# The second layer's gate/up projection as seven half-size products per block, with GpSimd forming the weight sums

## The reference

```python
D_FF = 2816
def conv_ffn(h, w_in, conv_w, conv_b, w_out):
    z = h @ w_in                                   # (512, 1024) @ (1024, 5632)
    g = dwconv(z[..., :D_FF], conv_w, conv_b)      # width 3 along the tokens
    return (jax.nn.silu(g) * z[..., D_FF:]) @ w_out
```

## Time and profile before

| | us |
|---|---|
| median of 3 runs | 1748.97 |
| span of the profiled execution | 1744.6 |
| TensorE busy | 1699.8 (97%), 9234 matmuls |
| VectorE busy | 1102.7 (63%) |
| ScalarE busy | 683.5 (39%) |
| GpSimd busy | 195.1 (11%) |
| granted TensorE clock, mean | 0.997 |

### The profile page before, as it was taken

The page is one execution under the profiler, slowest core; times in us unless marked ns, Lnnn a source line. Parts: engine busy times, 40 slices in busy tenths (PEclk is TensorE's granted clock), DMA queues, the critical chain, the costliest instruction groups (busy, mean ns, idle before and its releaser), DMA issues.

```text
span 1744.6 us, 23609 instructions
## 1 busy us (share of the span) xinstructions
PE 1699.8 (97%) x9234; PEld 1454.8 (83%) x9234; DVE 1102.7 (63%) x1745; ACT 683.5 (39%) x1127; POOL 195.1 (11%) x201
## 2 busy tenths in 40 slices
PE   6999999999999999999999999999999999999998
PEld 4788899787988888888888898879887888888777
DVE  5676777767676766644344678978875644444454
ACT  4343266544422221223344444454455422223442
POOL 1078500002100000000000210111210200000000
PEclk9999999999999999999999999999999999999999
DMA  8633000131334345441312122200012222222321
GB/s 343 215 124 116 17 22 1 75 143 49 133 128 162 138 152 193 169 134 55 114 50 95 40 102 80 97 1 1 33 42 86 95 73 96 97 97 97 131 98 71
DMA packets 40769, 173.08 MB, mean 99 GB/s; under 512 B 12640, under 2 KB 13152, under 8 KB 26208
## 3 DMA queue, kind: packets, MB, share of 16 engines
q1 hardware_dynamic: 31984, 166.75, 26.5%
q10 hardware_dynamic: 8688, 4.99, 1.0%
HBM read 169.60 MB, written 2.13 MB: 98 GB/s over the span
## 4 chain that ended last, share of the span: by engine, by line
PE 87%; DVE 4%; ACT 3%; DVEq 2%; issue 1%; DMA 1%; POOL 1%; ACTq 0%; SPq 0%; another core or an unknown queue 0%
PE PS L297 14%; PE PS L293 14%; PE PS L301 14%; PE PS L608 8%; PE PS L614 8%; PE PS L611 8%; PE PS L1120 4%; PE PS L325 3%; PE PS L328 3%; PE PS L329 3%; PE PS L1105 2%; DMA mod_raw<-modw 1%; DVE w_lo L282 1%; DVEq L1165 1%; ACT w_hi L276 1%
## 5 line engine op out<-in xcount | busy, mean ns | idle before, releaser
L293 PE MATMUL PS<-HT,w_hi 128*128 128x512 f32 (+1 forms) x1248 | 375.6, 347 | 0.0
L297 PE MATMUL PS<-HT,w_hi 128*128 128x512 f32 (+1 forms) x1248 | 375.5, 347 | 0.0
L301 PE MATMUL PS<-HT,w_lo 128*128 128x512 f32 (+1 forms) x1248 | 372.1, 344 | 0.0
L282 DVE TENSOR_TENSOR w_lo<-w_raw,w_hi 128x2048 fp32r<-128x2048 f32 x100 | 231.4, 2314 | 168.4 <-ACT w_hi L276 162.3
L608 PE MATMUL PS<-w_hi,a_ring 128*128 128x512 f32 x670 | 262.8, 392 | 2.9 <-DVE w_lo L282 0.9
L611 PE MATMUL PS<-w_lo,a_ring 128*128 128x512 f32 x670 | 260.9, 389 | 0.0
L276 ACT ACTIVATE w_hi<-w_raw 128x2048 fp32r<-128x2048 f32 x99 | 188.9, 1908 | 160.9 <-PE PS L608 103.7
L301 PEld LDWEIGHTS PS<-HT,w_lo 128*128 128x128 f32 x1248 | 211.7, 189 | 31.9
L293 PEld LDWEIGHTS PS<-HT,w_hi 128*128 128x128 f32 x1248 | 209.5, 188 | 29.9
L297 PEld LDWEIGHTS PS<-HT,w_hi 128*128 128x128 f32 x1248 | 210.6, 189 | 28.5
L988 DVE SCALAR_TENSOR_TENSOR yb<-PS,cws,yb 128x511 f32<-128x511 f32 (+1 forms) x132 | 83.1, 658 | 155.4 <-ACTq L949 151.0
(11 more groups left out here) (321 smaller groups left out, 2660.0 us busy)
## 6 DMA issues: line engine op xcount, KB each, us to landing
w_raw<-wpack SPq DMA_DIRECT2D x102, 1024.0 KB, 4.8
m_raw<-modu SPq DMA_DIRECT2D x80, 512.0 KB, 4.3
mod_raw<-modw SPq DMA_DIRECT2D x8, 1024.0 KB, 11.7
c_rows<-c_scratch SPq DMA_DIRECT2D x6, 512.0 KB, 5.2
X<-x SPq DMA_DIRECT2D x2, 1024.0 KB, 6.5
out<-X SPq DMA_DIRECT2D x4, 512.0 KB, 2.6
X<-ctx SPq DMA_DIRECT2D x1, 1024.0 KB, 10.0
gmB<-gate_rows_evo ACTq DMA_DIRECT2D x1, 1024.0 KB, 4.5
```

The source lines that it names most:

```text
L282: nc.vector.tensor_tensor(w_lo[r][:, :], w_raw[r][:, :], w_hi[r][:, :].bitcast(F32), ALU.subtract).then_inc(wl_ready, 1)
L293: mm = nc.tensor.matmul(o, wh, xh, start=start, stop=False)
L297: mm = nc.tensor.matmul(o, wh, xl, start=False, stop=False)
L301: last = nc.tensor.matmul(o, wl, xh, start=False, stop=stop)
```

## The change

The projection's slots 2 to 21 are computed by a Strassen scheme (seven products in place of eight). The weights of a slot are seen as a 2x2 block matrix: gate and up tile (m) by even and odd feature tiles (k), each block 4 feature tiles of 128 x 128, so 512 elements a partition. The activations are a 2x2 block matrix too: even and odd feature tiles by the first and second half (128) of each token group of 256. A product multiplies one weight matrix with one activation matrix, 4 feature tiles x 3 matmuls of 256 columns. Three products use a raw weight block (`RAW_OF`), four use a sum of blocks (`SUM_OF`), and so do the activations.

- GpSimd forms the four weight sums of each slot, `Sw0` to `Sw3`, from `w_raw` (`form_sum`).
- ScalarE makes the seven high parts `FH0` to `FH6` (`form_hi`), VectorE the seven low parts `FL0` to `FL6` (`form_lo`), 512 elements each. They lie where `w_hi` and `w_lo` lay, one buffer for each product, so that a high part waits for the same product of the slot before.
- The four activation sums ("turned") are formed once in each token group, for group 0 by GpSimd and for group 1 by VectorE (`turned_sum`), and split like the others (`TH`, `TL`). They are formed in place of the scaled activations, which for this norm now have 16 tiles of their own (`h_pre3`) in place of a ring of 6.
- Products share PSUM halves: products 3 and 6 accumulate onto product 0's bank "x" and product 4 onto product 1's bank "y". ScalarE copies out what must be kept before (`seven_keep`: p1, p5, u2, p4, in that order), and TensorE waits for p1 before product 3, p5 before product 4 and u2 before product 6.
- VectorE adds what was kept to what is in PSUM: gate sum `Gf`, up sum `up`. The convolution then reads `Gf` in SBUF and not PSUM.
- The loops over slots are unrolled, some semaphores are merged, and the output projection ffo1 uses banks 4 to 7.

The diff, cut to the new functions that matter here:

```diff
+        SUM_OF = {1: 0, 3: 1, 4: 2, 6: 3}
+        RAW_OF = {0: (0, 0), 2: (1, 0), 5: (1, 1)}
+        TURNED = (0, 2, 1, 3)
+        SPLIT = (0, 2, 1, 3, 4, 5, 6)
+        def formed(s, i):
+            return 6 * s + SPLIT.index(i) + 1
...
+        def form_sum(pool, s, j):
+            n = F11 + 2 + s
+            a11, a12, a21, a22 = (raw_part(n, k, m) for m in range(2) for k in range(2))
+            i = (1, 3, 4, 6)[j]
+            if j == 0:
+                raw_landed(pool, n)
+            if s:
+                if i == 6:
+                    pool.wait_ge(wl_ready, n)
+                else:
+                    pool.wait_ge(S("sv", "lo"), formed(s - 1, i))
+            pool.drain()
+            x, y, op = ((a21, a22, ALU.add), (Sw[0][:, :, :], a11, ALU.subtract), (a12, Sw[1][:, :, :], ALU.subtract),
+                        (a11, a21, ALU.subtract))[j]
+            nc.gpsimd.tensor_tensor(Sw[j][:, :, :], x, y, op).then_inc(S("sv", "sum"), 1)
+        def form_hi(act, s, i):
+            if i in SUM_OF:
+                act.wait_ge(S("sv", "sum"), 4 * s + SUM_OF[i] + 1)
+            else:
+                raw_landed(act, F11 + 2 + s)
+            if s:
+                product_done(act, s - 1, i)
+            else:
+                act.wait_ge(w_used, F11 - 1 if i < 4 else F11 + 2)
+            nc.scalar.activation(FH[i][:, :, :], form_source(s, i), ACT.Copy)\
+                .then_inc(wh_ready if i == 6 else S("sv", "hi"), 1)
+        def form_lo(dve, s, i):
+            if i == 6:
+                dve.wait_ge(wh_ready, F11 + 2 + s + 1)
+            else:
+                dve.wait_ge(S("sv", "hi"), formed(s, i))
+            nc.vector.tensor_tensor(FL[i][:, :, :], form_source(s, i), FH[i][:, :, :].bitcast(F32), ALU.subtract)\
+                .then_inc(wl_ready if i == 6 else S("sv", "lo"), 1)
...
+        def turned_sum(eng, ops, g, t):
+            if t == 0:
+                eng.wait_ge(S("pre3", "hi"), since("pre3", "hi") + KD * (g + 1))
+                eng.wait_ge(S("pre3", "lo_even"), since("pre3", "lo_even") + KD // 2 * (g + 1))
+            if t == 1:
+                eng.wait_ge(S("pre3", "lo_odd"), since("pre3", "lo_odd") + KD // 2 * (g + 1))
+            eng.drain()
+            b11, b12, b21, b22 = (half_tokens(g, k, h) for k in range(2) for h in range(2))
+            x, y = ((b12, b11), (b22, b11), (b22, b12), (b21, b22))[t]
+            ops.tensor_tensor(turned_place(g, t), x, y, ALU.subtract).then_inc(S("sv", f"tsum{g}"), 1)
...
+        def seven_pe(pe):
+            first_slots(pe, "pre3", F11, 2)
+            for s in range(JF - 2):
+                ns = s + 2
+                def bank(what):
+                    return PS[:, seven_bank(ns, what), 0:256]
+                for i in range(7):
+                    if i == 6:
+                        pe.wait_ge(wl_ready, F11 + ns + 1)
+                    else:
+                        pe.wait_ge(S("sv", "lo"), formed(s, i))
+                    if i == 0:
+                        if s < 2:
+                            pe.wait_ge(S("ff1", "evac"), since("ff1", "evac") + s + 1)
+                        else:
+                            pe.wait_ge(S("sv", "up"), s - 1)
+                    if s == 0 and i in (1, 3, 5):
+                        pe.wait_ge(S("sv", "tlo"), {1: 2, 3: 6, 5: 8}[i])
+                    if s == 0 and i == 5:
+                        pe.wait_ge(S("ff1", "evac"), since("ff1", "evac") + 2)
+                    if i in (3, 4, 6):
+                        pe.wait_ge(S("sv", "kept"), 4 * s + {3: 1, 4: 2, 6: 3}[i])
+                    o = bank(("x", "y", "w", "x", "y", "z", "x")[i]).rearrange("p (g c) -> p g c", g=2)
+                    for q in range(KD // 2):
+                        if i in (0, 2, 4):
+                            k, h = {0: (0, 0), 2: (1, 0), 4: (1, 1)}[i]
+                            xh, xl = (HT[:, 0:2, part, 2 * q + k, h * P:(h + 1) * P] for part in range(2))
+                        else:
+                            t = {1: 0, 3: 1, 5: 3, 6: 2}[i]
+                            xh, xl = TH[t][:, q, :, :], TL[t][:, q, :, :]
+                        begins, ends = q == 0 and i in (0, 1, 2, 5), q == KD // 2 - 1
+                        onto = i in (3, 4, 6)
+                        nc.tensor.matmul(o, FH[i][:, q, :], xh, start=begins, stop=False, skip_group_check=onto)
+                        nc.tensor.matmul(o, FH[i][:, q, :], xl, start=False, stop=False, skip_group_check=onto)
+                        last = nc.tensor.matmul(o, FL[i][:, q, :], xh, start=False, stop=ends, skip_group_check=onto)
+                    last.then_inc(w_used if i == 6 else S("sv", "prod"), 1)
+        def seven_keep(act, s, which):
+            ns = s + 2
+            what, i, dst = {"p1": ("x", 0, pu[:, 0, :]), "p5": ("y", 1, zp[:, 1, :]), "u2": ("x", 3, pu[:, 1, :]),
+                            "p4": ("z", 5, zp[:, 0, :])}[which]
+            product_done(act, s, i)
+            if s and which == "p1":
+                act.wait_ge(S("sv", "gate"), s)
+            if s and which == "p5":
+                act.wait_ge(S("sv", "up"), s)
+            nc.scalar.activation(dst, PS[:, seven_bank(ns, what), 0:256], ACT.Copy).then_inc(S("sv", "kept"), 1)
...
+            for s in range(JF - 2):
+                ns, last = s + 2, s == JF - 3
+                def next_hi(i):
+                    if not last:
+                        form_hi(act, s + 1, i)
+                seven_keep(act, s, "p1")
+                next_hi(0)
+                seven_keep(act, s, "p5")
+                next_hi(2)
+                next_hi(1)
+                if last:
+                    act.wait_ge(S("ff1", "evac"), since("ff1", "evac") + JF - 1)
+                    part(0)
+                    part(1)
+                seven_keep(act, s, "u2")
+                next_hi(3)
+                if last:
+                    round_hi(act, F21)
+                act.wait_ge(S("sv", "gate"), s + 1)
+                act.wait_ge(S("ff1", "evac"), since("ff1", "evac") + ns - 1)
+                conv_tap(ns, Gf[:, :])
+                next_hi(4)
+                seven_keep(act, s, "p4")
+                next_hi(5)
+                silu(ns)
+                next_hi(6)
+            act.wait_ge(w_used, F21)
+            part(2)
+            round_hi(act, F21 + 1)
...
+            for s in range(JF - 2):
+                ns, last = s + 2, s == JF - 3
+                def next_lo(i):
+                    if not last:
+                        form_lo(dve, s + 1, i)
+                for i in SPLIT[:4]:
+                    next_lo(i)
+                if last:
+                    part(0)
+                dve.wait_ge(S("sv", "kept"), 4 * s + 3)
+                product_done(dve, s, 4)
+                w = seven_bank(ns, "w")
+                nc.vector.tensor_tensor(by_half(Gf[:, :]), pairs(PS[:, w:w + 2, 0:256]), pairs(pu[:, :, :]), ALU.add)\
+                    .then_inc(S("sv", "gate"), 1)
+                dve.drain()
+                next_lo(4)
+                conv(ns, Gf)
+                next_lo(5)
+                if last:
+                    take_lo(dve, F21)
+                dve.wait_ge(S("sv", "kept"), 4 * s + 4)
+                product_done(dve, s, 6)
+                if last:
+                    part(1)
+                x = PS[:, seven_bank(ns, "x"), 0:256].unsqueeze(1).to_broadcast([P, 2, 256])
+                nc.vector.tensor_tensor(by_half(up[:, :]), pairs(x), pairs(zp[:, :, :]), ALU.add).then_inc(S("sv", "up"), 1)
+                next_lo(6)
+                dve.drain()
+                gated(ns, up[:, :])
+            part(2)
+            take_lo(dve, F21 + 1)
+        def seven_pool(pool):
+            for j in (0, 1):
+                form_sum(pool, 0, j)
+            for t in (1, 3):
+                turned_sum(pool, nc.gpsimd, 0, t)
+            for j in (2, 3):
+                form_sum(pool, 0, j)
+            for s in range(1, JF - 2):
+                for j in range(4):
+                    form_sum(pool, s, j)
...
+                form_hi(act, 0, 0)
+                form_hi(act, 0, 2)
...
+                for t in (0, 2):
+                    turned_sum(pool, nc.gpsimd, 0, t)
...
-            ffn_act(act, "ff1", 1, F11, LAT, lambda q: part_hi(act, "ffo1", q, JF, LT, A_ff_lat))
+            seven_act(act, lambda q: part_hi(act, "ffo1", q, JF, LT, A_ff_lat))
-            ffn_pe(pe, "ff1", F11, LAT, False, "pre3")
+            seven_pe(pe)
-            ffn_dve(dve, "ff1", 1, F11, LAT, A_ff_lat, False, lambda q: part_lo(dve, "ffo1", q, JF, LT, A_ff_lat))
+            seven_dve(dve, lambda q: part_lo(dve, "ffo1", q, JF, LT, A_ff_lat))
```

160 lines of the change are left out of this document (132 added, 28 removed).

## The result

The changed kernel takes 1788.6 us (median of 4 runs, 1785.6 to 1790.9). The kernel before takes 1748.3 beside it (1747.0 to 1749.8). The ratio is 1.0234, with an interval of 1.0219 to 1.0248: 40 us slower. That is on the side and inside the range that the prediction gives (1752 to 1798), but 13 us above its 1776. The profiled executions differ by 42.0 us (1786.6 against 1744.6).

The account below looks back on a forecast made before the run. TensorE bounds the projection before; afterwards the ScalarE-VectorE ring, with two GpSimd collisions, sets 12.0 us a slot against 10.88. 20 slots give +22.4, plus 1, 1 and 2.4: +27, to 1776 us, range 1752 to 1798.

Parts of the forecast that it names:

- TensorE's 10.08 a slot: Slots 2 to 21: 84 matmuls of 256 columns at 0.120 us make 10.08 us, against 10.88 before.
- The undisturbed ring: In each slot, ScalarE and VectorE hand work to and fro in program order: 10.2 us without any disturbance.
- Turns between GpSimd's reads and VectorE's: In the slots, GpSimd sums and VectorE two-input instructions exclude each other in SBUF; a collision delays VectorE about 0.9 us.
- In two-operand instructions: The prediction's condition for turns: GpSimd and VectorE both reading SBUF in two-operand instructions; no separate size.
- I walk one slot: ... 12.0: One new slot followed: two collisions on the ring, at the second convolution step and low 2, 10.2 + 1.8 = 12.0 us.
- the rival of three collisions: In the slots, GpSimd also gets turns between back-to-back VectorE instructions: 12.9 us a slot, total 1797; chance 0.21.
- the run of 24: Earlier trace: 24 gapless VectorE instructions kept a GpSimd product out, 3.69 us in all; cited against three collisions.
- TensorE's wait: Expected sign in the slots: TensorE idle some 1.9 us each, mostly at product 3's first matmul, released by ScalarE's keep.
- (a): Prenorm: GpSimd's two turned sums delay VectorE's xn or its 2.29 us low part, +1 us.
- (b): Before product 0: VectorE's 19 added instructions, 13.0 us, barely fit, with GpSimd's sums between them: +1 us.
- (c): Last slot: the first output slot's 2.29 us low part sits between convolution and up sum, +2.4 us.
- The sum: Whole kernel: 20 x (12.0 - 10.88) = +22.4, +1, +1, +2.4, together +27 us, median 1776.

Follow-up runs that it names:

- tiny sums: Changed kernel with each of GpSimd's four weight sums cut to one column per feature tile from slot 3 on (wrong weights): 1741.3 us, ratio 0.9965.
- short loads: Changed kernel with each slot's load of raw weights bringing only 128 of 2048 columns (wrong results): 1773.7 us, one run.
- GpSimd's turned sums tiny: Changed kernel with GpSimd's turned activation sums ahead of product 0 cut to one column per feature tile (wrong results): 1786.8 us, one run.

## Why the prediction was right in sign and short in size

- **TensorE's 10.08 a slot**: right. 10.08 where nothing disturbs it, with 84 matmuls at a pitch of 0.120.
- **The undisturbed ring, 10.2**: too long. With tiny sums TensorE has no idle time at 10.08, and VectorE has 0.6 us of slack in a slot, so the ring is 9.5 at most. I had added up lengths, and they overlap: low parts of 0.69 follow each other 0.60 apart (1512.28, 1512.89 in that run), and ScalarE's high parts and keeps overlap likewise.
- **Turns between GpSimd's reads and VectorE's, at about 0.9 on VectorE each**: right, in mechanism and size (1.03, 0.87, 1.11). GpSimd's sums average 1.53 to 1.59 us, over 1.29; I had said above 1.6 for a mean. "In two-operand instructions" was too narrow: the scaling of Pod in the earlier trace rows has one tensor input, and so has the copy that GpSimd's sums hold up in the kernel before.
- **"I walk one slot: ... 12.0"**: the step that failed. I had two collisions on the ring, at the second convolution step and at low 2. There are three, the third at the first step, and a slot is 12.65 long. That is the rival of three collisions (12.9 and 1797, chance 0.21), less the slack; the measured time is inside the range because the range took that rival in, and not because the forecast's slot was right. Two causes are shown. The first sum was not free to start under the gate sum: it waits for its load (63.6 us over 18 slots), since the load is issued behind low 6. With short loads the first step's collision vanishes and the slot takes 11.73. And GpSimd does get a turn between two VectorE instructions that follow without a gap (low 4 to step 1, the final product to low 0); I had read the run of 24 at 113.06 in the earlier trace rows as a rule. The same trace speaks against it ten microseconds later, where VectorE has no gap and six of GpSimd's products still follow each other at 1.72 to 1.73 us each (122.78 to 132.95). The 24 were instructions of 128 elements; here each is 512 wide. Whether the width makes the difference wasn't tried. Two neighbours of that stretch of the kernel before:

```profile
127.21 1.76 DVE L415 SCALAR_TENSOR_TENSOR m_raw<-m_raw,c_rows 128x1024 f32<-128x1024 f32 x1
127.85 1.73 POOL L1358 TENSOR_TENSOR sB<-Zq,csn 128x256 f32<-128x256 f32 x1
```

- **TensorE's wait**: as said, at product 3, released by ScalarE's keep, 1.84 us a slot (1.9 predicted). I said that it would be most of the idle time; in the slots it is all of it. The 29.4 us that the list of waits gives for TensorE's weight loads are the same waits, seen at the same matmuls: for the wait that ends at 1524.52 the low part that product 3 needs had been made at 1516.6, and the keep ended at 1524.37.
- **(a) the prenorm, +1**: right in size.

```profile
1375.47 1.77 POOL L673 TENSOR_TENSOR h_pre<-h_pre 128x512 f32<-128x512 f32 x1 [0.16 <-issue]
1376.14 3.25 DVE L297 TENSOR_TENSOR w_lo<-w_raw,w_hi 128x2048 fp32r<-128x2048 f32 x1
1377.40 3.13 POOL L673 TENSOR_TENSOR h_pre<-h_pre 128x512 f32<-128x512 f32 x1 [0.16 <-issue]
```

  The low part takes 3.25 beside the turned sums, 2.29 before: 0.96.
- **(b) ahead of product 0, +1**: too small.

```profile
1385.09 6.28 DVE L673 TENSOR_TENSOR h_pre<-h_pre 128x512 f32<-128x512 f32 x4 [0.17 <-DVE HT L494]
1391.30 3.49 DVE L652 TENSOR_TENSOR FL<-w_raw,FH 128x512 fp32r<-128x512 f32 x2
...
1402.19 0.55 PE L722 MATMUL PS<-HT,FH 128*128 128x256 f32 x1 [4.19 <-DVE A_ff_lat L812]
```

```profile
1385.88 1.54 POOL L631 TENSOR_TENSOR Sw<-w_raw 128x512 f32<-128x512 f32 x1 [0.16 <-issue]
```

  Four turned sums take 6.28 us, in place of 2.5 (an estimate, from a pitch of 0.60 where nothing disturbs), and the next two low parts 3.49, in place of 1.28: VectorE loses some 6 us. From 1385.88 to 1395.93 GpSimd makes six sums of 1.54 with 0.16 between them, and one VectorE instruction fits between each two. TensorE waits 4.19. I had priced the 19 instructions, and the turns between them hardly at all. The runs bear that out. From VectorE's second xn to product 0 it is 26.85 us here and 21.54 before; with GpSimd's turned sums tiny it is 24.63, and with memsets for the weight sums, where VectorE has the same 19 instructions, 22.50. In this execution VectorE's xn stood 1.35 us earlier than in the earlier trace rows, so the start cost 3.96 + 1.35 = 5.3 where (a) and (b) said 2.
- **(c) the last slot, +2.4**: right, 2.69. The low part named there ends at 1657.14, and TensorE starts at 1657.23:

```profile
1654.85 2.29 DVE L297 TENSOR_TENSOR w_lo<-w_raw,w_hi 128x2048 fp32r<-128x2048 f32 x1
```

- **The sum**: from product 0 on I had 22.4 + 2.4 = 24.8 and it is 37.4; the start 2 and 4.0; the rest 0 and 0.6. The excess of 15 us is 20 x 0.62 on the slots, 2.0 at the start, 0.3 in the last slot and the 0.6.
